# Second block's decay in four steps, its activations reordered, and the steps of the second block placed anew

## The chip, the cores and the metric

The kernel runs on one core of one Trainium2 chip. The metric is the device time of one execution in microseconds (us), lower being better, given as a median of several runs. TensorE is written PE, VectorE DVE, ScalarE ACT, GpSimd POOL and SyncE SP, as in the profile.

## What is computed

One sequence of 256 tokens of width 1024 passes through two blocks of two layers each. Only the second block is touched by the change. Cut to what matters, one of its layers is

```python
def hybrid_layer(x, ...):
    h = rmsnorm(x, norm_w)
    proj = h @ w_in                      # 3752 columns
    y_mla = mla_mixer(...) * silu(m_gate)      # latent attention
    y_gdn = gdn_mixer(...)                     # gated delta rule
    y_moba = moba_mixer(...) * silu(c_gate)    # block attention with a T5 bias
    return x + concatenate([y_mla, y_gdn, y_moba]) @ w_out

def gdn_mixer(q, k, v, z, b, a, conv_w, A_log, dt_bias, norm_w):
    qkv = silu(causal_conv(concatenate([q, k, v]), conv_w))   # four taps
    q, k = l2norm(q) * 128**-0.5, l2norm(k)
    beta = sigmoid(b)
    g = -exp(A_log) * softplus(a + dt_bias)
    o = chunk_gated_delta_rule(q, k, v, beta, g)
    return rmsnorm(o, norm_w) * silu(z)
```

The delta rule needs, for 4 heads and 256 tokens, the running sum of g (gc), its exponentials, and the matrices exp(gc_i - gc_j). The making of these is the "decay" of the title. Softplus is computed as max(y, 0) + ln(1 + exp(-|y|)).

## The kernel before

**Programs and semaphores.** Each engine has a program written out by hand: `tensor`, `scalar`, `vector`, `gpsimd`, `sync`. They meet through semaphores only: `put(name, key)` (L153) notes the count that a semaphore has after an instruction, and `e.wait_ge(*at(key))` on another engine waits for that count. An engine runs its program strictly in order, so whatever stands behind a waiting instruction waits as well.

**Parts.** The weights come as loads into a ring of three slots (SP, `issue`, L2662), each load cut into parts (`parts`, L371). Of each part j ACT makes the rounded copy `whi` (`split_hi`, L1130) and DVE the remainder `wlo` (`split_lo`, L1708), each with four buffers, so that PE can form an fp32 product as three products: high weight times high input, high times low, low times high. `split_hi(j)` waits until PE has done the first half of part j-4, `split_lo(j)` until PE has done the second half of part j-4 and until `whi` of part j is there. SP sends load i once `wlo` of the parts of load i-3 is made. A part of eight 128x256 products costs PE three groups of eight matmuls.

**Order within a layer of the second block.** `two_p` (L1039) walks through the parts 0 to 40: kc 0-3, ba 4, qc 5-8, m0 9-12, vc 13-16, cqk 17-20, cvg 21-24, mg 25-28, z 29-32, and the output product 33-40. All the other work of the layer is cut into tasks (bias, taps, others, decay, delta, latent, outs), each a generator whose `yield n` stands ahead of step n. `TWO_PLAN` (L92) gives each step a place. On PE place 2j lies in the middle of part j, behind its high products (`between`), and place 2j+1 behind the part (`behind`). On ACT and DVE the same plan is read with a distance: place 2j, then the split of part j+4, then place 2j+1 (`two_a`, L1604; `two_v`, L2509). POOL (`two_g`, L2644) walks through the places alone. At one place the tasks run in the order of the plan (bias, taps, others, decay, delta, latent, outs). Since 2j+1 and 2j+2 lie next to each other on ACT and DVE, a move between them changes only PE's order. No task's step issues a DMA.

**The decay** (`decay_p` L791, `decay_a` L1466, `decay_v` L2259). Step 0, place 10: PE turns the 8 rows of b and a into columns (L461), DVE copies them (L2263) and adds the bias (L2267, `t4a`). ACT takes the sigmoid of b (beta, L1469), |t4a| (L1471), Exp (L1473), Ln (L1475) and the Exp of A_log (L1476). DVE waits for that last one, forms softplus (L2270) and g (`gv`, L2272). Step 1, place 12: PE multiplies `gv` with a triangle of ones ("gsum", L456 on `st`), DVE copies the sum (L2278) and takes a difference (`edl`, L2280), ACT takes two exponentials (L1480, L1482). Step 2, place 17: PE turns gc, broadcast, into rows (`gcT`, L461 on `st`), first waiting for `edl`; DVE forms the differences `Dm` (L2285, L2289), ACT their exponentials (L1487).

**Other steps that the prediction speaks of.** taps: DVE convolves (L2239, L2242), ACT takes the sigmoid (L1462), DVE multiplies (L2255). delta 0, place 21: ACT squares k (L1551), PE sums the squares against a column of ones (L456, 128x1), DVE adds (L2349 for q, L2379 for k) and POOL takes the root. delta 1 to 3, place 23: DVE forms `r1` (L2385), PE the scores and the turned `r1` (`r1T`), DVE the products. delta 4, place 26: DVE `BT` (L2406), PE turns it. delta 5: PE turns k, DVE scales it (L2425). others 1: PE's second scores, DVE L2354, L2356, L2342. latent 4: PE turns q and k of the latent attention, ACT copies them (L1534). PSUM banks of kind "s" are handed out in rotation over four; who takes one waits until its last reader has left it.

Places are set by this, and a plan is read by

```python
                def between(j):
                    return lambda: side.run(TWO_AT.get(2 * (j - two0(l)), ()))

                def behind(j):
                    side.run(TWO_AT.get(2 * (j - two0(l)) + 1, ()))
```

Of the kernel before, what the change touches and what calls it, by code (L numbers as in the profile page):

```python
# [73 lines left out]
def two0(l):  # L74
# [17 lines left out]
TWO_PLAN = {  # L92
        "bias": [5, 5, 10, 20],
        "taps": [11, 11, 22, 23, 35, 41],
        "others": [27, 27, 43, 46, 50],
        "decay": [10, 12, 17],
        "delta": [21, 23, 23, 23, 26, 34, 37, 38, 39, 40, 42, 45, 46, 47, 47, 47, 48, 49, 51, 52, 52, 56, 58, 66, 68],
        "latent": [26, 29, 31, 31, 35, 37, 39, 41, 42, 42, 52, 60, 66],
        "outs": [62, 66, 68, 73],
}  # L100
# [33 lines left out]
class Values:  # L134
# [11 lines left out]
    def up(self, name):  # L146
        self.count[name] += 1
        return self.sems[name], 1
# [7 lines left out]
    def at(self, *key):  # L156
        return self.table.get(key, (None, 0)) if self.first else self.table[key]
# [23 lines left out]
def build(nc, a, out):  # L181
    ctx = ExitStack()
    with ctx:
# [267 lines left out]
        def tensor(e):  # L451
# [339 lines left out]
            def decay_p(l):  # L791
                yield 0
                bk = ps.take(e, "s", "bg", l)
                e.wait_ge(*at("rows8", l))
                for tb in range(2):
                    done = turn(bk[:, 8 * tb:8 * tb + 8], rows8[:, cols(tb)])
                done.then_inc(*up("decay.p"))
                put("decay.p", "bg", l)
                yield 1
                bk = ps.take(e, "s", "gsum", l)  # L800
                e.wait_ge(*at("gv", l))
                for tb in range(2):
                    group(bk[:, 4 * tb:4 * tb + 4], [(con("tri"), gv[:, tb])])
                group(bk[:, 8:12], [(onesb[:, :], gv[:, 0])]).then_inc(*up("decay.p"))
                put("decay.p", "gsum", l)
                yield 2
                for tb in range(2):
                    bk = ps.take(e, "s", "gcT", l, tb)
                    if tb == 0:
                        e.wait_ge(*at("edl", "in", l))  # L810
                    for h in range(4):
                        done = turn(bk[:, cols(h)], gc[:, tb, h:h + 1].to_broadcast([P, P]))
                    done.then_inc(*up("decay.p"))
                    put("decay.p", "gcT", l, tb)
# [312 lines left out]
        def scalar(e):  # L1127
# [338 lines left out]
            def decay_a(l):  # L1466
                yield 0
                e.wait_ge(*at("bg", "in", l))
                e.activation(beta, bg[:, :, 0:4], ACT.Sigmoid).then_inc(*up("decay.a"))  # L1469
                e.wait_ge(*at("t4a", l))  # L1470
# [4 lines left out]
                e.activation(t4b, t4b, ACT.Ln, bias=1.0).then_inc(*up("decay.a"))  # L1475
                e.activation(ea, prm("alog", l), ACT.Exp).then_inc(*up("decay.a"))  # L1476
                put("decay.a", "ea", l)
                yield 1
                e.wait_ge(*at("edl", "in", l))
# [3 lines left out]
                put("decay.a", "edl", l)  # L1483
                yield 2
                for tb in range(2):
# [221 lines left out]
        def vector(e):  # L1707
# [551 lines left out]
            def decay_v(l):  # L2259
# [7 lines left out]
                e.tensor_tensor(t4a, bg[:, :, 4:8], bc(prm("dtb", l), [P, 2, 4]), ALU.add).then_inc(*up(name))  # L2267
                put(name, "t4a", l)
                e.wait_ge(*at("ea", l))
                e.scalar_tensor_tensor(out=t4a, in0=t4a, scalar=0.0, in1=t4b, op0=ALU.max, op1=ALU.add).then_inc(*up(name))  # L2270
# [3 lines left out]
                put(name, "gv", l)  # L2274
                yield 1
                bk = bank("gsum", l)
# [5 lines left out]
                put(name, "edl", "in", l)  # L2282
                yield 2
                for tb in range(2):
# [520 lines left out]
```

## Time and profile before

| | us |
|---|---|
| median of 3 runs | 1435.99 (1434.65 to 1436.74) |
| the profiled execution, its own time | 1432.65 |
| its span in the profile | 1430.8 |
| PE busy, share of the span | 1371.6, 96% |
| DVE busy | 1072.6, 75% |
| ACT busy | 749.0, 52% |
| first layer of the second block | 1015 to 1222 |
| second layer of the second block | 1222 to the end |

A row of the timeline has start, length, engine, line, operation and tiles, and in brackets how long the engine stood idle before it and which instruction ended that. All instants below are us from the span's start. "w" in a row is any tile in the large work buffer, "st" the small statistics tile, "bank" a PSUM bank.

### The profile page before, as it was taken

What the parts mean: (1) busy time and instruction counts of PE and PEld (TensorE: products, weight loads), DVE (VectorE), ACT (ScalarE), POOL (GpSimd) and SP (SyncE); (2) the same over time, 40 slices, a digit from 0 to 9 for tenths busy, and PEclk for the clock granted to TensorE, in tenths of its full rate; (3) what the DMA queues carried; (4) which work ended last, traced back from release to release, by engine and by line L of the source; (5) the groups of instructions that cost most, each with busy time, mean ns of one, the idle gap of its engine ahead of it and who ended that gap; (6) DMA issues with size and microseconds to landing.
All of it is one profiled execution on the core that took longest, in us unless ns stands there. A gap on an engine that the chain in (4) does not pass through costs nothing.

```text
span 1430.8 us, 25396 instructions
## 1 busy us (share of the span) xinstructions
PE 1371.6 (96%) x10226; PEld 1290.7 (90%) x10226; DVE 1072.6 (75%) x1844; ACT 749.0 (52%) x1147; POOL 67.0 (5%) x62
## 2 busy tenths in 40 slices
PE   7999999999999999999999999999978999889998
PEld 6899999998999988999999989999778899788996
DVE  6899898667766768998986677667668557687556
ACT  6454656645544454546565564445553536654353
POOL 0000000000000000000000000000001210002210
PEclk9999999999999999999999999999989999989999
DMA  7565354564655545653545555555532114431121
GB/s 268 177 205 177 121 171 155 173 214 169 203 183 204 169 163 179 204 176 120 164 163 175 202 177 190 198 194 167 195 118 74 45 60 149 155 119 60 60 89 74
DMA packets 108844, 223.89 MB, mean 156 GB/s; under 512 B 6036, under 2 KB 17556, under 8 KB 108600
## 3 DMA queue, kind: packets, MB, share of 16 engines
q1 hardware_dynamic: 106352, 218.93, 46.1%
q10 hardware_dynamic: 2376, 3.35, 0.7%
q8 instruction: 81, 1.33, 0.4%
q14 instruction: 35, 0.29, 0.1%
HBM read 221.21 MB, written 1.06 MB: 155 GB/s over the span
## 4 chain that ended last, share of the span: by engine, by line
PE 39%; DVE 6%; ACT 3%; issue 2%; DMA 1%; POOL 0%; ACTq 0%; DVEq 0%; POOLq 0%
PE bank L481 13%; PE bank L456 8%; PE bank L490 7%; PE bank L503 5%; PE bank L511 2%; DVE wlo L1715 1%; DVE w L2242 1%; PE bank L461 1%; PE bank L526 1%; ACT whi L1140 1%; DMA ring<-in_w_in 1%; PE bank L1108 1%; PE bank L1111 1%; ACT hhi L1175 1%; PE bank L533 0%
## 5 line engine op out<-in xcount | busy, mean ns | idle before, releaser
L1715 DVE TENSOR_TENSOR wlo<-ring,whi 128x1024 fp32r<-128x1024 f32 (+3 forms) x430 | 496.7, 1177 | 187.2 <-ACT whi L1140 168.5
L1140 ACT ACTIVATE whi<-ring 128x1024 fp32r<-128x1024 f32 (+3 forms) x430 | 433.5, 1025 | 380.1 <-PE bank L481 236.8
L481 PE MATMUL bank<-hhi,whi 128*128 128x256 f32 x2016 | 281.4, 282 | 6.8 <-ACT sgb L1398 4.8
L490 PE MATMUL bank<-hhi,wlo 128*128 128x256 f32 x2016 | 280.5, 281 | 0.0
L481 PE MATMUL bank<-hlo,whi 128*128 128x256 f32 x2016 | 275.9, 279 | 0.0
L481 PEld LDWEIGHTS bank<-hhi,whi 128*128 128x128 f32 x2016 | 255.1, 190 | 11.1 <-ACT sgb L1398 5.5
L490 PEld LDWEIGHTS bank<-hhi,wlo 128*128 128x128 f32 x2016 | 253.7, 190 | 1.5 <-issue 1.3
L481 PEld LDWEIGHTS bank<-hlo,whi 128*128 128x128 f32 x2016 | 252.3, 190 | 0.0
L456 PE MATMUL bank<-w 128*128 128x128 f32 (+5 forms) x928 | 132.9, 296 | 5.3 <-ACT w L1534 3.6
L456 PEld LDWEIGHTS bank<-w 128*128 128x128 f32 (+2 forms) x928 | 116.2, 192 | 13.6 <-issue 4.4
L503 PE MATMUL bank<-whi,hhi 128*128 128x512 f32 (+2 forms) x256 | 98.4, 386 | 0.0
L1893 DVE SCALAR_TENSOR_TENSOR w<-w,par 128x256 f32<-128x256 f32 x240 | 98.0, 477 | 0.0
L503 PE MATMUL bank<-whi,hlo 128*128 128x512 f32 (+2 forms) x256 | 97.6, 382 | 0.0
L2575 POOL TENSOR_TENSOR st<-st,mhalf 128x1 f32<-128x1 f32 (+2 forms) x34 | 33.4, 982 | 1253.1 <-DVE st L1736 572.4
L511 PE MATMUL bank<-wlo,hhi 128*128 128x512 f32 (+2 forms) x256 | 66.5, 383 | 0.0
L503 PE MATMUL bank<-whi,flo 128*128 128x512 f32 x160 | 62.6, 392 | 0.0
L503 PE MATMUL bank<-whi,fhi 128*128 128x512 f32 x160 | 62.6, 391 | 0.0
L503 PEld LDWEIGHTS bank<-whi,hhi 128*128 128x128 f32 x256 | 49.0, 191 | 8.9 <-issue 0.9
L503 PEld LDWEIGHTS bank<-whi,hlo 128*128 128x128 f32 x256 | 49.2, 192 | 7.6
L511 PEld LDWEIGHTS bank<-wlo,hhi 128*128 128x128 f32 x256 | 48.3, 192 | 8.1
L511 PE MATMUL bank<-wlo,fhi 128*128 128x512 f32 x160 | 43.2, 392 | 0.0
L1570 ACT ACTIVATE w<-bank 128x512 f32<-128x512 f32 x24 | 14.1, 598 | 48.3 <-PE bank L456 48.3
(301 smaller groups left out, 1592.7 us busy)
## 6 DMA issues: line engine op xcount, KB each, us to landing
ring<-in_w_in SPq DMA_DIRECT2D x100, 1024.0 KB, 5.1
ring<-in_w_ffn_down SPq DMA_DIRECT2D x22, 1024.0 KB, 5.0
ring<-in_w_ffn_gate SPq DMA_DIRECT2D x20, 1024.0 KB, 5.1
ring<-in_w_ffn_up SPq DMA_DIRECT2D x20, 1024.0 KB, 5.0
ring<-in_w_merge SPq DMA_DIRECT2D x8, 1024.0 KB, 5.1
ring<-in_w_out SPq DMA_DIRECT2D x8, 1024.0 KB, 5.0
ring<-in_w_oc SPq DMA_DIRECT2D x4, 1024.0 KB, 5.1
ring<-in_w_od SPq DMA_DIRECT2D x4, 1024.0 KB, 5.1
```

The source lines that it names most:

```text
L456: done = e.matmul(o, l_, r_, start=start and i == 0, stop=stop and i == len(pairs) - 1)
L461: return e.transpose(o, i_, ident[0:n, 0:n])
L481: done = e.matmul(o, wh[:, k, cols(u)], s_[:, k0 + k, :], stop=False, skip_group_check=True, start=opens and k == 0 and s_ is sh and u % 2 ...
L490: done = e.matmul(o, wl[:, k, cols(u)], sh[:, k0 + k, :], start=False, stop=closes, skip_group_check=True)
L503: done = e.matmul(held[u][:, 0:n], s_[:, k0 + k, cols(u)], wh[:, k, 0:n], stop=False, start=opens and k == 0 and s_ is sh, skip_group_chec ...
L511: done = e.matmul(held[u][:, 0:n], sh[:, k0 + k, cols(u)], wl[:, k, 0:n], start=False, stop=closes, skip_group_check=True)
L526: done = e.matmul(acc[nh][tb][:, :], s_[:, k0 + k, cols(tb)], wh[:, k, :], start=False, stop=False, skip_group_check=True)
L1108: done = e.matmul(hv[u][:, 0:256], s_[:, k0 + k, cols(u)], w_[:, k, 0:256], start=begins, stop=closes and half_ == 1, skip_group_check=True)
L1140: e.activation(part_of(whi, j), part_raw(j), ACT.Copy).then_inc(*up("hi.a"))
L1715: e.tensor_tensor(part_of(wlo, j), part_raw(j), part_of(whi, j), ALU.subtract).then_inc(*up("lo.v"))
L1893: e.scalar_tensor_tensor(out=cacc[:, c], in0=glup[:, c, j:j + S], scalar=wv, in1=cacc[:, c], op0=ALU.mult, op1=ALU.add).then_inc(*up(name))
L2575: e.tensor_tensor(dst, src, half(n), ALU.pow).then_inc(*up(name))
```

## The change

Nothing that is computed changes. The decay gets four steps: step 0 as before as far as `t4a`; on DVE a step 1 of its own from the wait for `ea` to `gv`; the former steps 1 and 2 are now 2 and 3. On ACT the Exp of A_log comes first and beta's sigmoid last, behind the mark that DVE waits for. The decay's places 10, 12, 17 become 10, 10, 17, 17, so that PE's gsum product stands at place 17, right ahead of the gcT turns, and DVE's second part at place 10, right behind its first. Other steps move: bias 0 and 1 from 5 to 6, bias 2 from 10 to 21, bias 3 from 20 to 21; taps 3 from 23 to 26, taps 4 from 35 to 34, taps 5 from 41 to 35; others 1 from 27 to 34, others 2 from 43 to 42, others 3 from 46 to 48; delta 5 from 34 to 29, delta 21 from 56 to 55, delta 24 from 68 to 67; latent 4 from 35 to 36, latent 8 from 42 to 43, latent 9 from 42 to 44, latent 11 from 60 to 61, latent 12 from 66 to 64; outs 0 from 62 to 59, outs 2 from 68 to 67, outs 3 from 73 to 67.

```diff
--- before.py
+++ after.py
@@ -90,13 +90,13 @@
         "short": [89, 89, 94, 97],
 }
 TWO_PLAN = {
-        "bias": [5, 5, 10, 20],
-        "taps": [11, 11, 22, 23, 35, 41],
-        "others": [27, 27, 43, 46, 50],
-        "decay": [10, 12, 17],
-        "delta": [21, 23, 23, 23, 26, 34, 37, 38, 39, 40, 42, 45, 46, 47, 47, 47, 48, 49, 51, 52, 52, 56, 58, 66, 68],
-        "latent": [26, 29, 31, 31, 35, 37, 39, 41, 42, 42, 52, 60, 66],
-        "outs": [62, 66, 68, 73],
+        "bias": [6, 6, 21, 21],
+        "taps": [11, 11, 22, 26, 34, 35],
+        "others": [27, 34, 42, 48, 50],
+        "decay": [10, 10, 17, 17],
+        "delta": [21, 23, 23, 23, 26, 29, 37, 38, 39, 40, 42, 45, 46, 47, 47, 47, 48, 49, 51, 52, 52, 55, 58, 66, 67],
+        "latent": [26, 29, 31, 31, 36, 37, 39, 41, 43, 44, 52, 61, 64],
+        "outs": [59, 66, 67, 67],
 }
 
 
@@ -796,14 +796,14 @@
                     done = turn(bk[:, 8 * tb:8 * tb + 8], rows8[:, cols(tb)])
                 done.then_inc(*up("decay.p"))
                 put("decay.p", "bg", l)
-                yield 1
+                yield 2
                 bk = ps.take(e, "s", "gsum", l)
                 e.wait_ge(*at("gv", l))
                 for tb in range(2):
                     group(bk[:, 4 * tb:4 * tb + 4], [(con("tri"), gv[:, tb])])
                 group(bk[:, 8:12], [(onesb[:, :], gv[:, 0])]).then_inc(*up("decay.p"))
                 put("decay.p", "gsum", l)
-                yield 2
+                yield 3
                 for tb in range(2):
                     bk = ps.take(e, "s", "gcT", l, tb)
                     if tb == 0:
@@ -1465,23 +1465,22 @@
 
             def decay_a(l):
                 yield 0
-                e.wait_ge(*at("bg", "in", l))
-                e.activation(beta, bg[:, :, 0:4], ACT.Sigmoid).then_inc(*up("decay.a"))
+                e.activation(ea, prm("alog", l), ACT.Exp).then_inc(*up("decay.a"))
                 e.wait_ge(*at("t4a", l))
                 e.activation(t4b, t4a, ACT.Abs).then_inc(*up("decay.a"))
                 e.wait_ge(*now("decay.a"))
                 e.activation(t4b, t4b, ACT.Exp, scale=-1.0).then_inc(*up("decay.a"))
                 e.wait_ge(*now("decay.a"))
                 e.activation(t4b, t4b, ACT.Ln, bias=1.0).then_inc(*up("decay.a"))
-                e.activation(ea, prm("alog", l), ACT.Exp).then_inc(*up("decay.a"))
                 put("decay.a", "ea", l)
-                yield 1
+                e.activation(beta, bg[:, :, 0:4], ACT.Sigmoid).then_inc(*up("decay.a"))
+                yield 2
                 e.wait_ge(*at("edl", "in", l))
                 e.activation(egc, gc, ACT.Exp).then_inc(*up("decay.a"))
                 put("decay.a", "egc", l)
                 e.activation(edl0, edl0, ACT.Exp).then_inc(*up("decay.a"))
                 put("decay.a", "edl", l)
-                yield 2
+                yield 3
                 for tb in range(2):
                     e.wait_ge(*at("Dm", "in", l, tb))
                     e.activation(Dm[:, tb], Dm[:, tb], ACT.Exp).then_inc(*up("decay.a"))
@@ -2266,13 +2265,14 @@
                 e.wait_ge(*now(name))
                 e.tensor_tensor(t4a, bg[:, :, 4:8], bc(prm("dtb", l), [P, 2, 4]), ALU.add).then_inc(*up(name))
                 put(name, "t4a", l)
+                yield 1
                 e.wait_ge(*at("ea", l))
                 e.scalar_tensor_tensor(out=t4a, in0=t4a, scalar=0.0, in1=t4b, op0=ALU.max, op1=ALU.add).then_inc(*up(name))
                 e.wait_ge(*now(name))
                 e.scalar_tensor_tensor(out=gv, in0=t4a, scalar=-1.0, in1=bc(ea, [P, 2, 4]), op0=ALU.mult,
                                        op1=ALU.mult).then_inc(*up(name))
                 put(name, "gv", l)
-                yield 1
+                yield 2
                 bk = bank("gsum", l)
                 e.wait_ge(*at("gsum", l))
                 e.tensor_copy(tflat(gc), bk[:, 0:8]).then_inc(*up(name))
@@ -2280,7 +2280,7 @@
                 e.tensor_tensor(edl0, bk[:, 8:12], gc[:, 0], ALU.subtract).then_inc(*up(name))
                 leave(name, "gsum", l)
                 put(name, "edl", "in", l)
-                yield 2
+                yield 3
                 for tb in range(2):
                     e.tensor_tensor(heads(LT[:, tb]), bc(gc[:, tb], [P, 4, P], 2), bc(con("ahead"), [P, 4, P]),
                                     ALU.add).then_inc(*up(name))
```

## Rows read from the trace of the kernel before

**Rows 1.** The page: busy time of the engines (share of the span), instructions.

```profile
PE 1371.6 (96%) x10226; PEld 1290.7 (90%) x10226; DVE 1072.6 (75%) x1844; ACT 749.0 (52%) x1147; POOL 67.0 (5%) x62
```

**Rows 2.** PE's waits, whole span: waiter, releaser, us in total, times, longest.

```profile
PE bank L456 <- DVE st L2272: 9.5, 2, 5.0
PE bank L456 <- ACT w L1551: 4.9, 2, 2.7
...
PE bank L456 <- ACT w L1534: 3.6, 2, 1.8
PE bank L461 <- DVE st L2385: 3.0, 2, 2.5
...
PE bank L461 <- DVE w L2425: 1.6, 2, 0.9
```

**Rows 3.** PE's timeline, second layer, from part 6 to place 26.

```profile
1244.24 1.10 PE L481 MATMUL bank<-hlo,whi 128*128 128x256 f32 x8
1249.91 0.99 PE L456 MATMUL bank<-st,cst 128*128 128x4 f32 x4 [4.56 <-DVE st L2272]
...
1251.18 2.05 PE L490 MATMUL bank<-hhi,wlo 128*128 128x256 f32 x8
...
1255.95 1.07 PE L490 MATMUL bank<-hhi,wlo 128*128 128x256 f32 x8
...
1259.58 1.03 PE L461 MATMUL bank<-cst,st 128*128 128x128 f32 x8
...
1267.85 2.49 PE L456 MATMUL bank<-onesb,w 128*128 128x1 f32 x16 [2.66 <-ACT w L1551]
...
1277.65 1.09 PE L461 MATMUL bank<-cst,st 128*128 128x128 f32 x8 [0.55 <-DVE st L2385]
...
1283.36 1.23 PE L461 MATMUL bank<-cst,w 128*128 128x128 f32 x8 [0.52 <-DVE w L2406]
```

**Rows 4.** ACT's timeline, second layer.

```profile
1244.60 0.21 ACT L1471 ACTIVATE st<-st 128x8 f32<-128x8 f32 x1
...
1246.35 1.28 ACT L1475 ACT_TABLE_LOAD   x1
...
1247.87 1.28 ACT L1476 ACT_TABLE_LOAD   x1
...
1249.27 0.88 ACT L1140 ACTIVATE whi<-ring 128x832 fp32r<-128x832 f32 x1
...
1267.08 1.14 ACT L1551 ACTIVATE w<-w 128x512 f32<-128x512 f32 x2
```

**Rows 5.** DVE's timeline, second layer.

```profile
1244.40 0.17 DVE L2267 TENSOR_TENSOR st<-st,par 128x8 f32<-128x8 f32 x1
...
1249.60 0.17 DVE L2272 SCALAR_TENSOR_TENSOR st<-st 128x8 f32<-128x8 f32 x1
...
1251.65 2.46 DVE L2242 SCALAR_TENSOR_TENSOR w<-w,par 128x256 f32<-128x256 f32 x6
1254.03 1.47 DVE L2255 TENSOR_TENSOR w<-w,sgb 128x512 f32<-128x512 f32 x2
...
1257.21 1.96 DVE L1715 TENSOR_TENSOR wlo<-ring,whi 128x832 fp32r<-128x832 f32 x2 [1.44 <-ACT whi L1140]
...
1262.97 0.69 DVE L2289 TENSOR_TENSOR w<-bank,w 128x512 f32<-128x512 f32 x1
```

**Rows 6.** Stretches of the first layer: length; busy PE, PEld, DVE, ACT, POOL; granted clock; DMA.

```profile
1045.00:1047.00 2.00, 0.40 (x2) 0.43 (x3) 0.46 (x3) 1.97 (x4) 0.00 (x0) 0.50 0.00 1
...
1053.00:1055.00 2.00, 2.00 (x15) 2.00 (x15) 1.10 (x2) 1.65 (x3) 0.00 (x0) 0.76 0.00 0
```

**Rows 7.** PE's timeline, first layer.

```profile
1057.19 1.03 PE L461 MATMUL bank<-cst,st 128*128 128x128 f32 x8
```

**Rows 8.** DVE's timeline, first layer, ahead of the decay's first copy.

```profile
1040.23 0.41 DVE L2224 COPY w<-bank 128x256 f32<-128x256 f32 x1
1040.68 0.29 DVE L2227 TENSOR_TENSOR w<-w,cst 128x128 f32<-128x128 f32 x1
```

## The prediction

> **What bounds the kernel now.** I read the page first. PE is busy 96% of the span, DVE 75% and ACT 52% [rows 1]: time is won where PE stands still or runs slowly, and work taken off DVE or ACT counts only if PE waits for it.
>
> The list of PE's waits comes next [rows 2]. The longest one that the change touches is gsum's wait for `gv` (L2272): 9.5 us in two waits, one in each layer. Four more are near: for the squares of k (L1551, 4.9), for the latent copies (L1534, 3.6), for `r1` (L2385, 3.0) and for the scaled k (L2425, 1.6).
>
> The timelines of the second layer then show what stands behind them. PE ends its high products of part 6 at 1245.34, idles 4.56 us, and turns to gsum at 1249.91 [rows 3]. DVE had `t4a` at 1244.57, yet `gv` only at 1249.77 [rows 5]. Between the two, ACT ran |t4a|, Exp, Ln and the Exp of A_log, with a table load of 1.28 us ahead of each of the last three, two of which are shown [rows 4]. The wait is those loads.
>
> The stall has a tail. In the first layer the granted clock is 0.50, that is 1.2 GHz of 2.4, from before gsum until 1053 or later [rows 6]. In the second layer the three groups of eight matmuls from 1251.18 to 1255.95 take 4.77 us, while the four from 1255.95 to 1259.58 take 3.63, or 0.91 each [rows 3]; so 2.0 us are lost to the low clock there.
>
> **The change, part by part (second layer).** *ACT's order.* The Exp of A_log waits for nothing, so it and its table load fall into ACT's idle time ahead of `t4a`. From 1244.60 there remain |t4a| 0.21, Exp 0.21 without a load, load 1.28 and Ln 0.21, in all 1246.55 with the small gaps. `gv` follows two DVE operations later, near 1246.95, against 1249.77: 2.8 earlier. Beta's sigmoid with its load costs 1.5 more before ACT can make `whi` of part 9: 1248.05 against 1249.27, only 1.2 earlier [rows 4]. The kc sigmoid behind it then finds its table loaded.
>
> The Trainium skill ("ScalarE: Activation LUTs", What ACT_TABLE_LOAD costs) gives a switch of tables as 1.28 us of load and 1.38 of drain, 2.66 in all; by it the two switches that leave the chain would be worth 5.3 and not 2.6. The trace decides: Ln's load starts at 1246.35 and the next at 1247.87, 1.52 apart with Ln inside, so no drain is seen.
>
> *gsum from place 12 to 17.* PE no longer stops in part 6. From 1245.34 it has seven groups (one of part 6, three each of parts 7 and 8) of 0.91: 6.35, hence 1251.7; gsum takes 1.27 (1249.91 to 1251.18) and ends near 1253.0. `gv` is ready long before.
>
> *The new wait.* Right behind gsum stand the gcT turns, which wait for `edl`, and DVE makes `edl` only when it reaches place 17, behind `wlo` of part 12. DVE's queue: `wlo` of part 9 starts at about 1248.9 (ACT's 1248.05 and 0.88); from there to the end of the kc taps and products it needs what it needed before, 5.3 (1250.2 to 1255.5), so 1254.2; parts 10, 11 and 12 take 0.98 each [rows 5], so 1257.15; copy and difference 0.35. gcT starts near 1257.55 instead of 1259.58: **2.0 won**, not 4.56. PE idles some 4.6 us in its new place, and I take the low clock to follow as it does now [rows 6]. Queued behind the wait on PE is part 9 and all after it.
>
> *Place 21.* PE: gcT 0.79, parts 9 and 10 at full clock 4.83, and 1.9 for a low clock over most of part 9: about 1265.1. ACT: `Dm` is complete 2.8 after `edl` at 1260.3 (before 1263.6 [rows 5]), then exponentials, qc copies and two parts; the second waits for the middle of PE's part 10, about 1263.9. Its 0.95 and the first square (0.77, from 1267.08 to PE's 1267.85) give 1265.6: 2.2 won, with a stall of 0.5 for 2.66. The sums of squares then run at full clock, 1.84 for 2.49, and end at 1267.45, 2.9 earlier.
>
> *taps 3 from 23 to 26.* `r1` follows the squares by 7.31 now (1270.34 to 1277.65). The qc products, two operations like L2289's 0.69 and overlapping a little, 1.3, leave that chain: r1T at 1273.5. But they return ahead of `BT`, and that chain stays at 13.0 (1270.34 to 1283.36). So PE turns `BT` at 1280.45: **2.9 won** up to here; the stall has moved from r1T to `BT`, where it is 1.8 and not 0.52 [rows 3].
>
> *others 1, delta 5, latent 4, taps 4 and 5.* The scores (PE 1.75, DVE 1.6) and the turning of k (PE 0.8) trade places; the sum on PE is nought. The scaled k is made well before the latent turns need its bank, so the 0.85 for L2425 goes. What is late next is others 1's product: vc's taps now stand before it on DVE, and two of the four latent turns wait for its banks, some 1.15. Half a part more between turns and ACT's copies hides the 1.79 for L1534. With 0.3 from a bank wait at place 31, the balance is 1.8. **Second layer: 4.7 to 4.8.**
>
> *First layer.* Here a bias copy and its addition, 0.70 [rows 8], also leave DVE ahead of `t4a`. The same count puts gcT at 1053.6 for 1057.19 [rows 7]: 3.6. Bias 2 and 3 fill the stall of place 21. `BT` comes 4.4 earlier, and with 1.9 behind it: **6.3**. Bias 0 and 1 wait no more for their DMA (0.9 on PE), but PE stops for DVE and ACT soon after, so I count nothing.
>
> *The rest costs nothing.* No step issues a DMA, so SP's queue only follows `wlo`; POOL's roots are used later than made. Steps beyond place 42 lie where PE waits for nothing; their cover is DVE and ACT running a part or more ahead. outs 3 delays two splits by about 1.3 while PE needs them 4 or more later; without that cover it would cost 1.3 a layer.
>
> **Sum.** 6.3 + 4.8 = 11.1. The profiled execution took 1432.65, 1.85 more than its span; the change would make it 1421.55. The median shown is 3.3 above that execution; 1435.99 - 11.1 = **1424.9**.
>
> Unknown from both sides: the low clock behind the new gap can be absent (+1.3 won in the second layer, +0.4 in the first) or last as long as the one shown in the first layer, at least 8 us [rows 6], which costs another 2.2 a layer; the stall at place 36 can be 0 or the present 1.8. I take the short low stretch, as the second layer shows it. These bounds alone give 1422 to 1431.
>
> **The rivals.** A difference of 0.2%, 2.9 us, is what a measurement of this kernel can tell from none.
>
> A: the stall closes altogether. It needs DVE at place 17 by 1253, 4.5 earlier than I count. The saving would be 9.5 of waits and about 5 of low clock (2.0 here, 3.0 in the first layer): 1421.5, and 1419 with part of the later stalls. Against it stand three remainders and 3 us of taps in DVE's queue. 0.13.
>
> B: the gain of the first half is swallowed. The chain of DVE and ACT up to the squares keeps its length, since ACT now has two fixed parts and the exponentials in one run, and only the 1.8 a layer behind `BT` is left: 1432.4. For it: PE waits for that chain today (L1551, L2385, L1534). 0.12, half of it under 0.2%.
>
> C: the Exp of A_log isn't free. If its table load is not over before `t4a`, or Exp is loaded again, `gv`, `whi` of part 9 and gcT come 1.3 to 1.5 later in each layer: 1427.8. Against it ACT idles over 3 us there. 0.05.
>
> D: Ln needs no load of its own, because the Exp loaded before it lies in the same table. `gv` and gcT would come 1.28 earlier a layer: 1422.3. Today's trace loads at Ln and again at the Exp behind it [rows 4], which speaks against. 0.03. The Trainium skill ("ScalarE: Activation LUTs", Table sets) states that one set holds both functions.
>
> E, **slower**: the gap in front of gcT outgrows the one removed. It decides once DVE reaches place 17 more than 2.0 (second layer) or 3.6 (first) later than counted, and two 8 us low stretches follow. With gcT 1 us later than today and 4 us of low clock where 2.0 and 3.0 are lost now, less the 3.7 behind `BT`: 1436 + 2 + 3 - 3.7 + 2 for a second low stretch at place 21, about 1439.5. Gaps of 2.66 at that place have lowered the clock already [rows 3]. 0.05.
>
> The rule that speaks against this change is that of "TensorE: Matmul & The Clock Gate" (HAM oscillation) in the Trainium skill: long idle gaps between bursts throttle TensorE anew each time. The trace agrees at 4.56 and 2.66 us.
>
> **How the numbers follow.** The forecast has 0.62, of which 0.01 within 0.2%. Faster: 0.61 + 0.13 + 0.06 + 0.05 + 0.03 = 0.88; same 0.01 + 0.06 = 0.07; slower 0.05. The range 1419 to 1431 takes in A, C, D and the bounds, and leaves out B and E.
>
> **What would show it.** In the profile after: a load at L1476 while ACT waits and none at L1473; gsum waiting for nothing, and a new wait of 4 to 5 us of L461 on DVE L2280 in each layer; low clock behind it; r1T without a wait or under 2, `BT`'s grown to about 1.8; L1534 gone from the list, a wait on L2342 of about 1. Wrong if L2280's wait is under 2 (rival A) or over 7 (E), or if the squares (L1551) still cost over 4 in all (B).

## The result, and the profile after

The changed kernel took 1425.65 us (median of 4 runs, 1423.88 to 1429.22) beside 1435.41 for the kernel before: a ratio of 0.9939, 95% interval 0.9925 to 0.9953, so 9.8 us by the medians. In a second group of runs, named after_again below, it took 1426.68 beside 1435.68, ratio 0.9942 (0.993 to 0.9954). Forecast were 1424.9 and a saving of 11.1.

The profiled execution happens to be the slowest of the four: 1429.22 us, span 1427.4. That of the kernel before, at 1432.65, lies 2.8 below its median, so the two profiles alone understate the gain. PE's and DVE's busy times are those of before to 0.3% [rows 1].

```profile
span 1427.4 us, 25394 instructions
...
PE 1374.8 (96%) x10226; PEld 1294.3 (91%) x10226; DVE 1072.4 (75%) x1844; ACT 746.6 (52%) x1145; POOL 68.0 (5%) x62
```

The list of PE's waits, changed kernel (waiter, releaser, us in total, times, longest), answers to [rows 2]:

```profile
PE bank L461 <- DVE st L2280: 10.7, 2, 5.6
...
PE bank L461 <- DVE w L2406: 3.4, 2, 1.7
...
PE bank L461 <- DVE w L2342: 2.0, 2, 1.1
...
PE bank L456 <- ACT w L1550: 1.2, 2, 1.0
...
PE bank L461 <- DVE st L2385: 0.9, 2, 0.5
```

The waits on L2272, L1534 and L2425 are gone, 14.7 us together. In their stead stand `edl` (L2280), 10.7, a longer wait for `BT` (L2406), 3.4 for 1.0, and one on the second scores' bank (L2342), 2.0 for 0.7. The squares' line is L1550 now; PE waits 1.2 us for it where it waited 4.9.

Next the timeline of PE in the second layer, as in [rows 3]. Its first row, the first turns of the layer, is the mark from which I measure; the kernel before has that row at 1223.39 (first layer: 1017.10), the changed one at 1219.36 (1019.09).

```profile
1219.36 1.18 PE L461 MATMUL bank<-cst,xn 128*128 128x128 f32 x8 [1.27 <-DVE xn L1755]
...
1247.78 0.51 PE L456 MATMUL bank<-st,cst 128*128 128x4 f32 x4
...
1253.66 1.94 PE L461 MATMUL bank<-cst,st 128*128 128x128 f32 x8 [5.15 <-DVE st L2280]
...
1262.39 1.92 PE L456 MATMUL bank<-onesb,w 128*128 128x1 f32 x16 [1.03 <-ACT w L1550]
...
1270.42 1.09 PE L461 MATMUL bank<-cst,st 128*128 128x128 f32 x8 [0.39 <-DVE st L2385]
...
1277.33 1.23 PE L461 MATMUL bank<-cst,w 128*128 128x128 f32 x8 [1.73 <-DVE w L2406]
...
1279.94 3.41 PE L456 MATMUL bank<-onesb,w 128*128 128x1 f32 x16
```

gsum (1247.78) waits for nothing. PE stands idle for 5.15 us ahead of the turns, which then take 1.94, where they took 1.03 before: the low clock. The wait for `BT` is 1.73.

ACT's timeline in the same layer (beside [rows 4]) has the Exp of A_log first, in time that was idle, and one load between `t4a` and `gv` where there were three:

```profile
1237.19 1.28 ACT L1468 ACT_TABLE_LOAD   x1
...
1240.62 0.21 ACT L1470 ACTIVATE st<-st 128x8 f32<-128x8 f32 x1 [1.93 <-DVE st L2266]
...
1241.09 1.28 ACT L1474 ACT_TABLE_LOAD   x1
...
1242.61 1.28 ACT L1476 ACT_TABLE_LOAD   x1
...
1244.02 0.89 ACT L1140 ACTIVATE whi<-ring 128x832 fp32r<-128x832 f32 x1
...
1251.90 1.28 ACT L1479 ACT_TABLE_LOAD   x1
1253.55 0.21 ACT L1479 ACTIVATE st<-st 128x8 f32<-128x8 f32 x1 [0.36 <-DVE st L2280]
...
1260.67 1.06 ACT L1140 ACTIVATE whi<-ring 128x1024 fp32r<-128x1024 f32 x1 [1.21 <-PE bank L503]
```

DVE's (beside [rows 5]) shows the queue that the turns wait for: three remainders, then the copy, then `edl`:

```profile
1242.62 0.17 DVE L2270 SCALAR_TENSOR_TENSOR st<-st 128x8 f32<-128x8 f32 x1 [2.04 <-ACT st L1474]
...
1250.34 2.90 DVE L1714 TENSOR_TENSOR wlo<-ring,whi 128x832 fp32r<-128x832 f32 x3
...
1253.35 0.16 DVE L2280 TENSOR_TENSOR st<-bank,st 128x4 f32<-128x4 f32 x1
...
1256.18 0.69 DVE L2289 TENSOR_TENSOR w<-bank,w 128x512 f32<-128x512 f32 x1
```

From mark to mark (one execution of each kernel), the first layer fell from 206.3 to 200.3 us, 6.0 saved. From the second mark to the end it is 207.4 before and 208.1 after: nothing saved in this execution. The stretch of 1276 to 1290 tells why. Here are the changed kernel and after_again (length; busy PE, PEld, DVE, ACT, POOL; granted clock; DMA share, GB/s):

```profile
1276.00:1290.00 14.00, 12.67 (x69) 12.52 (x70) 8.05 (x19) 3.35 (x7) 5.51 (x5) 0.63 0.25 77
```

```profile
1276.00:1290.00 14.00, 12.28 (x108) 11.93 (x107) 11.68 (x25) 7.02 (x19) 4.41 (x4) 1.00 0.29 85
```

Behind the wait for `BT` the clock was at its lower level (1.2 GHz) for some 10 us in the one and not at all in the other, although the code is the same. In the first of them q's sums of squares, at 1279.94, take 3.41 us; in after_again, at 1281.56, 1.84 (PE's timeline of after_again):

```profile
1255.54 1.94 PE L461 MATMUL bank<-cst,st 128*128 128x128 f32 x8 [5.34 <-DVE st L2280]
...
1264.63 1.92 PE L456 MATMUL bank<-onesb,w 128*128 128x1 f32 x16 [1.03 <-ACT w L1550]
...
1272.65 1.09 PE L461 MATMUL bank<-cst,st 128*128 128x128 f32 x8 [0.36 <-DVE st L2385]
...
1279.57 1.23 PE L461 MATMUL bank<-cst,w 128*128 128x128 f32 x8 [1.73 <-DVE w L2406]
...
1281.56 1.84 PE L456 MATMUL bank<-onesb,w 128*128 128x1 f32 x16
...
1290.44 4.46 PE L456 MATMUL bank<-w 128*128 128x384 f32 x12
```

after_again (marks at 1021.51 and 1221.08, span 1425.0) is 6.7 and 3.5 us shorter than before in its two layers, 10.2 in all where the other execution has 5.4. Which execution one profiles is worth nearly 5 us here. Nor do the marks agree: the first stands at 1017.10, 1019.09 and 1021.51, behind code of which no place was changed.

### The profile page after: what moved, and what is told of

Its sections match the earlier page's. It is cut to its first block, busy times and chain, and to the rows that moved or that the text cites. A ratio compares the mean times of both kernels' runs of the same rounds, so it can differ in the third digit from the quotient of the medians.

```text
span 1427.4 us, 25394 instructions
## 1 busy us (share of the span) xinstructions
PE 1374.8 (96%) x10226; PEld 1294.3 (91%) x10226; DVE 1072.4 (75%) x1844; ACT 746.6 (52%) x1145; POOL 68.0 (5%) x62
## 4 chain that ended last, share of the span: by engine, by line
PE 41%; DVE 5%; ACT 2%; issue 1%; DMA 1%; DVEq 0%; ACTq 0%; POOLq 0%; POOL 0%
PE bank L481 13%; PE bank L456 8%; PE bank L490 7%; PE bank L503 6%; PE bank L511 2%; PE bank L461 2%; DVE w L2241 2%; DVE wlo L1714 1%; ACT whi L1140 1%; PE bank L526 1%; PE bank L1108 1%; DMA ring<-in_w_in 1%; PE bank L1111 1%; PE bank L533 0%; DVE w L2238 0%
## 5 line engine op out<-in xcount | busy, mean ns | idle before, releaser
L2636 POOL TENSOR_TENSOR w<-w,cst 128x512 f32<-128x512 f32 x24 | 33.5, 1414 | 104.9 <-PE bank L456 104.9
```

The source lines that it names most:

```text
L2636: e.tensor_tensor(heads(BT[tb]), heads(LT[:, tb]), bc(con("lv", lv * P, lv * P + P), [P, 4, P]), ALU.mult).then_inc(*up("delta.g"))
```

## The experiments

Each kernel was compared with the kernel before, on the same chip. As times between groups differ by a few us, I go by the ratios. Their intervals are 0.001 to 0.0018 to either side, so two kernels whose ratios lie less than about 0.0018 (some 2.6 us) apart aren't shown to differ. Each kernel has one profiled execution. I held three theories. **Q**, the forecast's: a stall costs what it shows, and gsum's place and ACT's order can be summed from DVE's queue. **P**: the decay only moves its stall, and the other places bring the gain. **R**, formed after the first group: one chain through DVE and ACT, from `t4a` through taps, splits, `Dm`, exponentials and squares to `BT`, sets the pace, and PE waits somewhere along it whatever is done on PE.

| kernel | us | before | ratio (95%) |
|---|---|---|---|
| changed | 1425.65 | 1435.41 | 0.9939 (0.9925 to 0.9953) |
| after_again | 1426.68 | 1435.68 | 0.9942 (0.9930 to 0.9954) |
| decay_only | 1432.49 | 1435.45 | 0.9979 (0.9965 to 0.9994) |
| places_only | 1430.48 | 1435.45 | 0.9964 (0.9950 to 0.9978) |
| act_order_only | 1432.57 | 1435.45 | 0.9985 (0.9976 to 0.9995) |
| gsum_12 | 1429.32 | 1435.45 | 0.9961 (0.9945 to 0.9976) |
| old_act_order | 1429.01 | 1435.68 | 0.9960 (0.9946 to 0.9973) |
| middle_back | 1430.68 | 1435.68 | 0.9983 (0.9966 to 1.0001) |
| taps3_back | 1425.58 | 1435.68 | 0.9930 (0.9918 to 0.9942) |
| tail_back | 1425.07 | 1433.34 | 0.9941 (0.9928 to 0.9954) |
| fill_gap | 1423.04 | 1433.34 | 0.9929 (0.9914 to 0.9945) |
| late_q | 1455.11 | 1433.34 | 1.0146 (1.0131 to 1.0161) |
| fill_taps3 | 1423.89 | 1431.62 | 0.9943 (0.9925 to 0.9960) |

**after_again**: the changed kernel, unaltered.

> The changed kernel once more, unaltered, so that the kernels of this group have it beside them. Theory Q and theory R alike: the gain of 9.8 us over the kernel before comes again, 1425 to 1427. If the median comes out above 1428, the first four runs were lucky.

Measured: the gain came again, 9.0 us by the medians.

**decay_only**: the changed kernel's decay, every other step at its old place.

```diff
-        "decay": [10, 12, 17],
+        "decay": [10, 10, 17, 17],
```

(against the kernel before; the decay's lines in the programs are those of the changed kernel)

> The new decay (four steps, ACT's new order, places 10, 10, 17, 17), every other step at its old place. Theory Q (DVE's queue): the saving is what the turns at place 17 come earlier, less than the stall that goes: L2280's wait about 5 us in each layer, BT about 3 us earlier in the second layer and 4.4 in the first, the waits on L1534 and L2425 still there. Gain about 7 us, 1428.5. Rival P (places): the decay's stall only moves, and the gain comes from the other steps' new places; then 1433 to 1435 here.

Measured: 3 us faster than before by the ratio (0.9 to 5.0), not Q's 7; P's 1433 to 1435 is missed by half a us, which is within the noise. The waits came out as Q had them (L2280 10.0 in two, L1533 3.6, L2425 1.7):

```profile
PE bank L461 <- DVE st L2280: 10.0, 2, 5.2
...
PE bank L456 <- ACT w L1533: 3.6, 2, 1.8
PE bank L461 <- DVE st L2385: 3.3, 2, 1.7
```

In its profiled execution, the second fastest of 12 (1428.03 to 1437.66), `BT` is turned 4.7 and 2.6 us earlier from the mark, 7.3 in all, about what Q counted. The layers are 4.7 and 0.8 shorter, 5.5 in all. The difference lies in the second layer, behind the wait for the latent copies. Decay_only, then the kernel before:

```profile
1307.98 4.57 PE L456 MATMUL bank<-w 128*128 128x128 f32 x24 [1.80 <-ACT w L1533]
```

```profile
1314.01 2.94 PE L456 MATMUL bank<-w 128*128 128x128 f32 x24 [1.79 <-ACT w L1534]
```

The same 24 matmuls behind the same wait take 1.6 us more: the granted clock from 1308 to 1312 is 0.57 in decay_only and 1.00 in the kernel before. Q got the instants right and had no term for this. How often it happens one profile can't say.

**places_only**: the kernel before with the other steps' new places.

```diff
+        "taps": [11, 11, 22, 26, 34, 35],
+        "others": [27, 34, 42, 48, 50],
         "decay": [10, 12, 17],
```

(only the added lines; bias, delta, latent and outs likewise as in the change)

> The old decay (three steps, old order on ACT, places 10, 12, 17), all other steps at their new places. Theory Q: the wait on L2272 stays at about 4.7 us a layer with its low clock; only the middle relief is won, about 1.8 us a layer: 1432. The wait on L2406 grows to about 1.8 and that on L2385 shrinks by 1.3. Rival P: most of the 9.8 us is here, 1427 or less.

Measured: 5.2 us (ratio 0.9964), between Q's 3.6 and P's 8 or more. The decay and the places add: 0.9979 x 0.9964 = 0.9943, the changed kernel's own ratio. So both halves are real, at about 3 and 5 us, each to within 2.

**act_order_only**: three lines moved in the kernel before.

```diff
             def decay_a(l):
                 yield 0
+                e.activation(ea, prm("alog", l), ACT.Exp).then_inc(*up("decay.a"))
-                e.wait_ge(*at("bg", "in", l))
-                e.activation(beta, bg[:, :, 0:4], ACT.Sigmoid).then_inc(*up("decay.a"))
                 e.wait_ge(*at("t4a", l))
...
-                e.activation(ea, prm("alog", l), ACT.Exp).then_inc(*up("decay.a"))
                 put("decay.a", "ea", l)
+                e.activation(beta, bg[:, :, 0:4], ACT.Sigmoid).then_inc(*up("decay.a"))
```

> The kernel before with only ACT's order changed (Exp of A_log first, beta's sigmoid last); gsum stays at place 12. Theory Q: gv comes 2.8 us earlier, so gsum's wait falls from 4.7 to about 1.8 us a layer, DVE has edl done by the time PE reaches place 17, so no new wait stands there and no low clock follows; squares about 5.8 us earlier per layer; 1424, that is, as fast as the whole change or faster. Rival S (the split and place 17 are what matters): only the shorter wait is won, 2.8 us a layer, 1430.

Measured: 2.2 us by the ratio (0.7 to 3.4). Q had forecast 11 and failed clearly; rival S, with its 5.6, missed as well. gsum's wait shrank as said, to 2.6 in two, and the turns waited 0.3. But what PE gained it lost at the squares:

```profile
PE bank L456 <- ACT w L1550: 10.6, 2, 5.6
...
PE bank L456 <- DVE st L2271: 2.6, 2, 1.7
```

10.6 us where the kernel before waits 4.9 [rows 2]. Of the 6.9 us that the one wait lost, the other gained 5.7. PE had run ahead of DVE and ACT. And the new gap has its own low stretch, on the sums themselves: PE's timeline, second layer:

```profile
1254.52 1.06 PE L461 MATMUL bank<-cst,st 128*128 128x128 f32 x8 [0.27 <-DVE st L2279]
...
1265.69 3.54 PE L456 MATMUL bank<-onesb,w 128*128 128x1 f32 x16 [5.55 <-ACT w L1550]
```

The sixteen sums take 3.54 us and not 1.9, and `r1` waits for them. So theory R was formed. Its measure is the time from `t4a` on DVE to the first sum of squares on PE, first and second layer:

| kernel | from t4a to the squares, us |
|---|---|
| before | 24.4, 23.5 |
| places_only | 23.7, 23.4 |
| old_act_order | 23.9, 23.0 |
| changed; after_again | 22.0, 22.0; 22.7, 22.3 |
| decay_only | 22.1, 21.2 |
| act_order_only | 21.4, 21.4 |
| gsum_12 | 21.4, 21.4 |
| middle_back; taps3_back; tail_back | 22.5, 21.1; 21.4, 21.3; 21.6, 21.7 |
| late_q | 22.5, 22.0 |
| fill_gap; fill_taps3 | 20.1, 20.1; 20.1, 20.1 |

With gsum at place 12 and ACT's new order it is 21.4 in four layers of two kernels, while gsum's wait ranges from 0.9 to 2.3 us and a low stretch lies behind it in one of the four. So in these four PE's doings in between don't enter. With gsum at place 17 they do: changed, after_again, middle_back, taps3_back and tail_back run the same code up to the squares and need 21.1 to 22.7, and with the gap filled it is 20.1 four times. Nor does the chain alone give the time: act_order_only and gsum_12 have one that is no longer than the changed kernel's and are slower. What lies behind it, up to `BT` and beyond, counts too.

**gsum_12**: the changed kernel with gsum back at place 12.

```diff
-        "decay": [10, 10, 17, 17],
+        "decay": [10, 10, 12, 17],
```

> The changed kernel with one number altered: gsum (step 2 of the decay) at place 12 and not 17. Theory Q: it joins the 5.8 us a layer of ACT's order and the 1.8 of the middle steps: 1420, some 5 us faster than the changed kernel; wait on L2272 about 1.8 a layer, none on L2280. Rival S: taking gsum from 17 back to 12 costs a stall that the change had removed: 1427 or slower.

Measured: 0.9961 against 0.9939, so about 3 us slower than the changed kernel, though the intervals overlap a little. Q's 1420 failed; rival S has the direction. The chain to the squares isn't longer (21.4), but the idle time stands before the squares again, 7.4 us in all:

```profile
PE bank L456 <- ACT w L1550: 7.4, 2, 4.7
...
PE bank L456 <- DVE st L2272: 4.0, 2, 2.2
```

At place 17 a gap is followed by turns and a part for which PE has time, at place 21 by sums for which DVE waits: in the first layer these took 3.54 us behind a gap of 4.7, in the second 1.92 behind one of 2.8. That this makes the 3 us is argued, not shown: from the mark, `BT` comes at 60.98 and 57.63 here, at 60.32 and 57.97 in the changed kernel and at 59.62 and 58.49 in after_again.

**old_act_order**: the changed kernel with ACT's old order.

```diff
                 yield 0
-                e.activation(ea, prm("alog", l), ACT.Exp).then_inc(*up("decay.a"))
+                e.wait_ge(*at("bg", "in", l))
+                e.activation(beta, bg[:, :, 0:4], ACT.Sigmoid).then_inc(*up("decay.a"))
...
+                e.activation(ea, prm("alog", l), ACT.Exp).then_inc(*up("decay.a"))
                 put("decay.a", "ea", l)
-                e.activation(beta, bg[:, :, 0:4], ACT.Sigmoid).then_inc(*up("decay.a"))
```

> The changed kernel with ACT's old order in the decay (beta's sigmoid first, Exp of A_log last), all else as changed. Theory R (DVE and ACT's chain from t4a through the splits to the squares and BT sets the pace, gsum's place doesn't): DVE waits 4.8 and not 2.0 us for ea, of which 1.3 to 1.5 reach the split of part 9 and all behind it; 3 us slower than the changed kernel. Rival F: all 2.8 us a layer count, 5.6 slower. Rival N: gsum at place 17 hides it whole, no difference.

Measured: 0.9960 against 0.9942 of after_again, 2.6 us slower; near theory R's 3. F's 5.6 is excluded, N's nought only just, the intervals overlapping. The traces support R: from the mark, `BT` comes 2.0 and 0.6 us later than in after_again, 2.6 in all. L2281 (the same `edl`) is waited for 13.4 us instead of 10.6:

```profile
PE bank L461 <- DVE st L2281: 13.4, 2, 6.9
```

**middle_back**: the changed kernel with taps 4, 5, others 1, delta 5 and latent 4 at their old places.

```diff
-        "taps": [11, 11, 22, 26, 34, 35],
-        "others": [27, 34, 42, 48, 50],
+        "taps": [11, 11, 22, 26, 35, 41],
+        "others": [27, 27, 42, 48, 50],
```

(and delta 5 from 29 to 34, latent 4 from 36 to 35)

> The changed kernel with the middle steps at their old places: taps 4 and 5 at 35 and 41, others 1 at 27, delta 5 at 34, latent 4 at 35. Theory R: the waits on L1534 (1.8 a layer) and L2425 (0.85) return and that on L2342 at the latent turns (1.0) goes: 1.8 us a layer, 3.6 slower than the changed kernel. Rival: these steps only trade stalls, under 1 us.

Measured: 0.9983 against 0.9942, 5.9 us by the ratios and 4.0 by the medians (two of its twelve runs took 1440.5 and 1441.4, which raises the ratio); the 3.6 is within the noise of both. The first two waits are back to the tenth:

```profile
PE bank L456 <- ACT w L1533: 3.6, 2, 1.8
...
PE bank L461 <- DVE w L2425: 1.6, 2, 0.9
...
PE bank L456 <- DVE w L2342: 0.9, 2, 0.5
```

By either count this is the largest single part of the change, though not clear of the noise. From `BT`'s turn to the first uq product it is 12.3 us in all eight layers with the old places (before, decay_only, act_order_only, middle_back) and 10.9 to 11.0 in 16 of 18 with the new ones (late_q left out), 1.4 a layer. In the profiled second layer the 24 matmuls behind L1533 took 4.57 here too, as in decay_only, so the old places can also cost a low stretch that the count of waits leaves out.

**taps3_back**: the changed kernel with taps 3 at place 23.

```diff
-        "taps": [11, 11, 22, 26, 34, 35],
+        "taps": [11, 11, 22, 23, 34, 35],
```

> The changed kernel with taps 3 (the qc products) back at place 23. Theory R: the sum of the waits on L2385 and L2406 stays, about 1.7 and 0.5 where it is 0.5 and 1.7; the time stays within 1 us, unless the place of the stall decides whether the clock falls behind it. Rival: the move is worth its 1.3 us a layer, 2.6 slower.

Measured: 0.9930 against 0.9942, within the intervals of each other: no loss, perhaps 1 to 2 us gained. The stall moved back as said (L2385 4.0, L2406 1.0):

```profile
PE bank L461 <- DVE st L2385: 4.0, 2, 2.4
...
PE bank L461 <- DVE w L2406: 1.0, 2, 0.5
```

So this move brings nothing.

**fill_gap**: 40 matmuls in the gap, their result overwritten.

```diff
                     if tb == 0:
+                        for _ in range(40):
+                            e.matmul(bk[:, 0:S], hhi[:, 0, 0:P], hhi[:, 0, :], start=True, stop=True,
+                                     skip_group_check=True)
                         e.wait_ge(*at("edl", "in", l))
```

> The changed kernel with 40 more matmuls of 128x256 on PE between gsum and the wait of the turns at place 17, written into the bank that the turns then overwrite; about 4.5 us at 0.113 us each, so they fit into the gap of 5.1 to 5.6. Theory C (the clock's fall behind the gap costs time): no low stretch starts there, the 2 us of slow turns and part 9 come back in each layer, 2 to 4 us faster than the changed kernel. Theory R: since DVE and ACT set the pace up to BT, most of that is swallowed by longer waits at the squares (1 becomes 2 to 3 us): under 1.5 us faster in all.

Measured: 0.9929; 1.9 us faster than the changed kernel by the ratios 0.9942 and 0.9929, between the two theories, with overlapping intervals. The trace is clearer. PE's timeline, second layer, and the clock of that stretch:

```profile
1247.42 5.04 PE L811 MATMUL bank<-hhi 128*128 128x256 f32 x40
1252.85 1.09 PE L461 MATMUL bank<-cst,st 128*128 128x128 f32 x8 [0.39 <-DVE st L2283]
...
1259.81 1.92 PE L456 MATMUL bank<-onesb,w 128*128 128x1 f32 x16 [1.33 <-ACT w L1553]
```

```profile
1247.00:1258.00 11.00, 10.61 (x77) 10.36 (x77) 9.34 (x18) 7.57 (x12) 0.00 (x0) 1.00 0.55 184
```

(L811 is the added line.) The matmuls fill the gap down to 0.39 us, the clock stays at 1.00, the turns take 1.09 and not 1.94, and the chain to the squares falls to 20.1 in both layers, from the changed kernel's 22.0 (21.1 to 22.7 in other profiles of that code): the low clock behind the gap costs 1 to 2.6 us of that chain, 2 in the middle, through the middle of part 10 for which ACT waits. So theory R doesn't hold as strictly as it was put: PE's clock is a part of the chain. Of some 4 us for two layers, less than half reach the time by the ratios. The profiled execution waits 2.4 for `r1` (0.9 and 2.3 in the changed kernel's two profiles) and 3.4 for `BT`; its layers are 0.5 and 2.0 us shorter than those of after_again.

**late_q**: q's work moved behind `BT`.

```diff
-        "taps": [11, 11, 22, 26, 34, 35],
-        "others": [27, 34, 42, 48, 50],
+        "taps": [11, 11, 27, 29, 34, 35],
+        "others": [31, 36, 42, 48, 50],
```

> The changed kernel with work on the q path taken off DVE's chain ahead of BT: taps 2 and 3 at 27 and 29 (22 and 26 before), others 0 at 31 (27), others 1 at 36 (34). Theory R: the chain from the sums of squares to BT is 4 us shorter, so the waits on L2385 and L2406 (about 2.2 a layer) go; 3 to 4 us faster than the changed kernel if DVE has room for them from place 27 on. Rival: DVE is late further down, the waits come back at the latent turns and the uq product (places 31 to 37), no gain or slower.

Measured: 21 us slower than the kernel before by the ratio, 22 by the medians. The waits on L2385 and L2406 did go (nothing and 1.0), but two of 10 us took their place, and the sums behind the first run at the low clock:

```profile
PE bank L456 <- DVE w L2425: 10.9, 2, 5.5
...
PE bank L461 <- DVE w L2342: 10.1, 2, 5.2
```

```profile
1308.46 3.57 PE L456 MATMUL bank<-onesb,w 128*128 128x1 f32 x16 [5.47 <-DVE w L2425]
```

At place 31 q's sums need a bank that DVE frees with L2425, and that stands in DVE's queue behind the taps at 27, their products at 29 and the sigmoid between them. DVE had no room there. The rival was right, and by far more than it said.

**tail_back**: everything from place 42 on at its old place.

```diff
-        "outs": [59, 66, 67, 67],
+        "outs": [62, 66, 68, 73],
```

(and others 2, 3, delta 21, 24, latent 8, 9, 11, 12)

> The changed kernel with everything from place 42 on at the old places: others 2 and 3 at 43 and 46, delta 21 and 24 at 56 and 68, latent 8, 9, 11, 12 at 42, 42, 60, 66, outs 0, 2, 3 at 62, 68, 73. The forecast counted these moves at nothing, since PE waits for nothing there: within 1 us of the changed kernel, and no new wait of PE. Rival: outs or latent moved earlier give PE a shorter stretch up to the output product; then 1 to 3 us slower here.

Measured: 0.9941, the changed kernel's ratio. No wait came or went: these eleven moves bring nothing that shows.

**fill_taps3**: the edits of fill_gap and taps3_back together.

> The two versions that came out ahead of the changed kernel joined: 40 more matmuls in the gap at place 17, and taps 3 back at place 23. If their gains add (1.9 us and 1.6 us by the ratios), 1422 beside a kernel before of 1435.5, a ratio near 0.9917. If the gain of taps 3 was only that the clock didn't fall behind BT, and the matmuls already see to that, the two don't add and the ratio stays at 0.993. Waits: L2385 1.6 to 2.4 and L2406 0.5 a layer, L2280 0.4.

Measured: 0.9943, interval 0.9925 to 0.9960. The gains don't add, and this group doesn't even confirm that of the filling. L2385's wait is 4.8 in two, and behind the longer one, 3.04 us in the first layer, the granted clock fell to 0.50:

```profile
PE bank L461 <- DVE st L2388: 4.8, 2, 3.0
...
PE bank L461 <- DVE w L2409: 1.0, 2, 0.5
```

(L2388 and L2409 are L2385 and L2406, three lines lower.) No version was shown to be faster than the changed kernel; fill_gap and taps3_back are the candidates, 1 to 2 us ahead and within the noise.

## Why the prediction was right, and where it wasn't

The direction, the mechanism and the size held: 9.8 and 9.0 us for 11.1. That the sum comes so close owes something to luck. The prediction had 7.3 up to `BT` and 3.8 behind it. By the ratios the decay's half brought 3.0 alone (decay_only) and the other places 5.2 (places_only): one too high, clear of its interval, the other perhaps too low. In the profiled executions `BT` comes 5.9 and 6.1 earlier over both layers (changed, after_again).

*ACT's order.* Forecast were |t4a|, Exp, load, Ln, and no load at the second Exp. So it is: 1240.62 to Ln's end takes 1.97, `gv`'s first operation waits 2.04 where it waited 4.83. Rivals C and D fall with the loads at L1468, ahead of `t4a`, and at L1474. `whi` of part 9 starts 3.60 after `t4a`'s row and not 4.87 [rows 4, 5], 1.3 earlier for 1.2. Worth about 2.6 us of the time (old_act_order, at the edge of the noise).

*What the split brought beside.* I hadn't counted one thing. At place 12 ACT loads the Exp table and takes the exponentials of `gc` and `edl` ahead of `whi` of part 10, for which DVE waits 1.44 [rows 5]; at place 17 both lie behind the splits, and DVE's three remainders follow each other without a wait (1250.34). That fits the chain of fill_gap, with no low clock in the way: 20.1 for the 21.4 of gsum at place 12.

*gsum and the new wait.* From the layer's mark the turns come at 34.30 where they came at 36.19, and in the first layer at 36.46 for 40.09: 1.9 and 3.6, forecast 2.0 and 3.6. The gap was put at 4.6 and is 5.15: I had taken 1.27 for gsum from a row at the low clock, and at the high one it takes 0.74. The low clock behind it came in both layers. With 10.7 us of waits on L2280 rival A falls, and with none over 5.6, E; the squares' 1.2 speaks against B, whose sign was over 4.

*The squares.* 2.2 was forecast, 1.4 came (44.46 to 43.03 from the mark). As foreseen, ACT waits there for the middle of PE's part 10, 1.21 us at 1260.67. That middle comes 7.0 us behind the start of the turns, where 6.35 was counted (1257.55 to 1263.9). The low clock costs 2.1 there, over the turns and most of part 9, for the 1.9 that I had put over part 9 alone. And I had set the middle of part 10 1.2 ahead of the part's end; the kernel before has 0.8 (1264.43 and 1265.19).

*`r1` and `BT`.* The chain from the end of the sums to r1T was put at 6.0 and is 6.1 (1264.31 to 1270.42). `BT` comes 2.0 earlier in the second layer (57.97 for 59.97), forecast 2.9, with a wait of 1.73 for 1.8. The last 0.9 is the squares' shortfall.

*The middle.* 1.8 a layer was forecast, and the waits changed as named: L1534 and L2425 gone, L2342 about 1.0. middle_back puts it at 4 to 6 us in all, with an uncertainty of 2 to 3.

*The first layer* was to save 6.3 and saved 6.0 and 6.7 in the two profiled executions.

**The step that failed** is the second layer's 4.8: it saved 3.5 in one execution and nothing in the other. Where it saved 3.5, `BT` came 1.5 earlier and not 2.9, and 2.0 were won behind it, as forecast. Where it saved nothing, the term for the clock was too small. I counted one low stretch, behind the new gap, and called the wait for `BT` 1.8 us and no more. It can cost 4.6 besides: the stretch from `BT`'s turn to the first uq product took 15.6 us in the one execution and 10.9 in the other. The same waits, of 5.2, 1.0, 0.4 and 1.7 close behind each other, stand in both executions, so what lets the clock fall in the one stays open. Of 18 layers with the new places (late_q left out) two took 15.6 and 15.7 there, the second in gsum_12. The upper bound for the low clock, 2.2 more a layer, was asked for at place 17 alone.

A second weakness showed only in the experiments. The forecast treated PE as the bound and its stalls as the price; act_order_only, forecast by the same count, missed by 9 us. decay_only missed as well, by 4 us. There the count gave `BT`'s instant (7.3 us earlier over both layers, 7.4 expected), and the price was wrong. So following DVE's and ACT's queues told when a wait ends; it didn't tell what the time would gain.

Still open is why 12 runs of one kernel spread over 4 to 14 us. Where the low stretches lie differs from one execution to the next, but only one execution of each kernel is profiled. A part of the spread is none of the change's: the first mark, behind code of which no place was moved, lies between 1015.82 and 1021.86 us in the fourteen profiles.

## What to carry to other kernels

When the busiest engine waits several times in a row for the same two others, follow the chain on those two before pricing a stall; here, removing one wait handed most of it to the next (act_order_only). If a wait must be, it looks better placed where the work behind it has slack, since that work may run at the lower clock (gsum_12 suggests this and doesn't prove it). Compare a kernel's parts by more than one profiled execution where you can: two of the same code differed by nearly 5 us. And a plan step moved into an engine's queue delays all that shares a bank with what stands behind it (late_q lost 29 us against the changed kernel, by the ratios, by four numbers).

## What the runs showed of the hardware

A table load on ACT can start ahead of the wait of the instruction that it serves: the load for the exponentials at place 17 ran at 1251.90 and ended 0.36 us before `edl` let them start, so a waiting instruction didn't hold back its own load. A load takes 1.28 us each time.

The granted clock fell to its lower level behind every gap of PE from 3.0 to 6.9 us in the second block, 28 of them in 13 of the fourteen profiles (fill_gap has none so long). Behind waits of 1.6 to 2.8 us it fell in some executions only: within a us behind one of 1.80, in gsum_12, decay_only and middle_back, and behind the 1.73 before `BT` in one of two executions of the same code (0.63 against 1.00 in the same 14 us). Forty matmuls whose result nobody reads kept it at 1.00 through the gap of 5 us.
